# A hybrid HGRN2/GLA decoder step on one core: sample turns in one pass, squares added on VectorE, scaling in pieces, conditioning tiles in batches of eight, and an output stage on two engines

## What is computed

```python
def trunk(x, c, ...):
    cs = silu(c)
    for l in range(2):
        sh1, sc1, g1, sh2, sc2, g2 = split(cs @ w_ada[l] + b_ada[l], 6)   # conditioning
        h = x * (1 + sc1) + sh1
        y, s = (hgrn2_mixer if l == 0 else gla_mixer)(h, ...)
        x = layer_norm(ALPHA * x + (1 + g1) * y)
        h = x * (1 + sc2) + sh2
        y = square(relu(h @ w_up[l])) @ w_down[l]
        x = layer_norm(ALPHA * x + (1 + g2) * y)

def gla_mixer(h, ...):
    q, k, v, g, low = split(h @ w_in)
    log_f = log_sigmoid(low @ w_gk2 + b_gk) / 16
    o, s = gated_linear_recurrence(q * 256**-0.5, k, v, log_f, s0)
    o = o * rsqrt(mean(o * o) + eps) * norm_w * silu(g)      # per head of 512 values
    return o @ w_out, s
```

## Time and profile before

| | us |
|---|---|
| median of 3 runs (lowest, highest) | 3125.11 (3121.99, 3128.86) |
| the profiled execution's own time | 3127.16 |
| its span, first to last instruction | 3125.4 |
| PE busy | 3049.0 (98%) |
| DVE busy | 1734.8 (56%) |
| ACT busy | 1307.9 (42%) |
| POOL busy | 294.0 (9%) |

### The profile page before, as it was taken

One profiled execution on the slowest core, in us unless ns is written; L12 is line 12 of the kernel. 1 busy time (PEld: TensorE's weight loads), 2 busy tenths in 40 slices (PEclk: granted clock), 3 DMA queues, 4 the chain that ended last, 5 costly groups with the idle time before them and its releaser, 6 DMA issues.

```text
span 3125.4 us, 66220 instructions
## 1 busy us (share of the span) xinstructions
PE 3049.0 (98%) x26988; PEld 2852.2 (91%) x26988; DVE 1734.8 (56%) x2471; ACT 1307.9 (42%) x1702; POOL 294.0 (9%) x290
## 2 busy tenths in 40 slices
PE   6899999999999999999999999999999999999998
PEld 3689999989899999999999889997999999999998
DVE  2476776665744444444445666666574444454446
ACT  1355555553433333333333544544353343343433
POOL 0022111111300000000001401110130000000000
PEclk9899999999999999999999999999999999999999
DMA  9998788888777676776775875675545555555552
GB/s 376 317 309 258 252 258 261 269 287 278 259 252 236 209 254 212 229 241 205 238 254 176 266 233 169 197 235 184 162 135 164 168 164 168 163 167 165 166 167 73
DMA packets 541633, 685.60 MB, mean 219 GB/s; under 512 B 22225, under 2 KB 469257, under 8 KB 541065
## 3 DMA queue, kind: packets, MB, share of 16 engines
q1 hardware_dynamic: 484402, 625.43, 61.7%
q10 hardware_dynamic: 56960, 56.21, 5.5%
HBM read 650.88 MB, written 30.67 MB: 218 GB/s over the span
## 4 chain that ended last, share of the span: by engine, by line
PE 74%; DVE 3%; DMA 1%; ACT 1%; issue 0%; SPq 0%; DVEq 0%; ACTq 0%
PE main L560 23%; PE main L562 22%; PE main L561 22%; PE bank L572 2%; PE bank L1154 1%; PE bank L1139 0%; DMA raw<-in_w_ada 0%; DVE z L2404 0%; DVE z L2408 0%; PE bank L1125 0%; DVE w_lo L1905 0%; PE bank L702 0%; ACT w_hi L1291 0%; PE bank L1191 0%; DVE a_lo L2438 0%; PE bank L590 0%
## 5 line engine op out<-in xcount | busy, mean ns | idle before, releaser
L1905 DVE TENSOR_TENSOR w_lo<-raw,w_hi 128x1024 fp32r<-128x1024 f32 x804 | 988.2, 1231 | 1187.0 <-ACT w_hi L1291 1183.1
L1291 ACT ACTIVATE w_hi<-raw 128x1024 fp32r<-128x1024 f32 x804 | 850.3, 1059 | 1508.4 <-PE main L562 1394.4
L560 PE MATMUL main<-a_hi,w_hi 128*128 128x288 f32 x4224 | 1276.8, 302 | 8.7 <-DVE a_lo L2438 6.0
L562 PE MATMUL main<-a_hi,w_lo 128*128 128x288 f32 x4224 | 1248.5, 296 | 0.0
L561 PE MATMUL main<-a_lo,w_hi 128*128 128x288 f32 x4224 | 1247.4, 295 | 0.0
L560 PEld LDWEIGHTS main<-a_hi,w_hi 128*128 128x128 f32 x4224 | 796.2, 188 | 49.7 <-issue 35.2
L561 PEld LDWEIGHTS main<-a_lo,w_hi 128*128 128x128 f32 x4224 | 795.7, 188 | 4.6 <-issue 1.9
L562 PEld LDWEIGHTS main<-a_hi,w_lo 128*128 128x128 f32 x4224 | 795.8, 188 | 0.0
L560 PE MATMUL main<-act_hi,w_hi 128*128 128x288 f32 x2048 | 606.3, 296 | 0.0
L562 PE MATMUL main<-act_hi,w_lo 128*128 128x288 f32 x2048 | 604.9, 295 | 0.0
L561 PE MATMUL main<-act_lo,w_hi 128*128 128x288 f32 x2048 | 601.9, 294 | 0.0
(11 more groups left out here) (321 smaller groups left out, 2053.4 us busy)
## 6 DMA issues: line engine op xcount, KB each, us to landing
raw<-in_w_ada SPq DMA_DIRECT2D x384, 512.0 KB, 6.7
raw<-in_w_up SPq DMA_DIRECT2D x256, 512.0 KB, 3.8
raw<-in_w_down SPq DMA_DIRECT2D x256, 512.0 KB, 3.5
raw<-in_hg_w_in SPq DMA_DIRECT2D x128, 512.0 KB, 6.5
raw<-in_gla_w_in SPq DMA_DIRECT2D x100, 512.0 KB, 4.3
raw<-in_hg_w_out SPq DMA_DIRECT2D x32, 512.0 KB, 7.9
gl_s<-in_state_gla ACTq DMA_DIRECT2D x32, 512.0 KB, 5.7
out_new_gla_sample<-gl_s ACTq DMA_DIRECT2D x32, 512.0 KB, 4.8
```

Of the source, the lines that this page charges most:

```text
L560: mm(out, hi, x_hi[:, kb, :], start=kb == 0, stop=False)
L562: last = mm(out, lo, x_hi[:, kb, :], start=False, stop=kb == KB - 1)
L1291: F(w_hi[:, st.split_slot(g)].rearrange("p k n -> p (k n)"), raw[:, slot, :], ACT.Copy).then_inc(hi_ready, 1)
L1905: V.tensor_tensor(w_lo[:, s].rearrange("p k n -> p (k n)"), raw[:, slot, :], w_hi[:, s].rearrange("p k n -> p (k n)").bitcast(F32), ALU.su ...
```

## The change

It has six parts.

1. The samples are turned in one pass. The three copies that the strips need are made ahead (DVE's key product and ACT's value copy write three copies, `threefold`), and one true transpose of 96 columns replaces three products. The scores buffer grows from 64 to 96 rows to match.
2. In GLA, DVE adds the four blocks of squares (two additions), and PE sums one block and not four, at step 11 and not 10.
3. DVE's multiplication by the reciprocal root moves from step 10 to step 13, and the four by weight and gate to steps 14 to 17.
4. In MLP0 the 32 conditioning tiles of an iteration come in 4 batches of 8 and not in 8 of 4, in the first iteration at steps 8, 12, 24 and 36.
5. In GL0 the last 8 conditioning tiles come together ahead of step 9 and not as 4 ahead of step 3 and 4 ahead of step 6; the gate's two products move from steps 10 and 11 to 11 and 12, and the load of `w_gk2` no longer stands behind the conditioning copy on ACT.
6. At the end 8 banks are used, ACT and DVE share the copies, DVE applies weight and bias to the last chunk, and SP stores 9 of the 12 pieces.

In the piece with `if s == 10` the engine is DVE.

```diff
-    MLP_OPENING += [("a", i) for i in range(32) if step == max(6 * (i // 4), 3)] + first_weights(step + 3, min(step + 4, 64))
+    MLP_OPENING += [("a", i) for i in range(32) if step == max(12 * (i // 8), 8)] + first_weights(step + 3, min(step + 4, 64))
-MLP0 = Stage(HGO, 4, 64, {s: 4 for s in range(0, 48, 6)}, "A" * 8 + "V" * 8, lead=KB, opening=MLP_OPENING)
+MLP0 = Stage(HGO, 4, 64, {s: 8 for s in range(0, 48, 12)}, "A" * 8 + "V" * 8, lead=KB, opening=MLP_OPENING)
-GL0 = Stage(MLP0, 1, len(GL_FIRST), {0: 8, 3: 4, 6: 4}, emptied_by="AAAAVV")
+GL0 = Stage(MLP0, 1, len(GL_FIRST), {0: 8, 9: 8}, emptied_by="AAAAVV")
...
-        def turn_samples(bank, at, src, copies=3):
-            for j in range(copies):
-                last = mm(bank[32 * j:32 * j + 32, at:at + P], src, ident[:, :], start=True, stop=True,
-                          skip_group_check=True, tile_position=(0, 32 * j))
-            return last
+        def turn_samples(bank, at, src):
+            return turn(bank[0:96, at:at + P], src.rearrange("p c t -> p (c t)"), ident[:, :])
...
         def hg_key_mul(n):
             dve.wait_ge(H["kd_exp"], n + 1)
+            step(V.tensor_tensor(hg_s3[:, 2:4], threefold(hg["x"][:, 1, :, TP:T]), threefold(hg["k"][:, :, TP:T]), ALU.mult))
...
         def gl_sum(n):
-            pe.wait_ge(G["squared"], n + 1)
+            pe.wait_ge(G["sq_summed"], n + 1)
             pe.wait_ge(G["ss_read"], 8 * n + 8)
-            for v in range(4):
-                last = mm(b5[:, 0:T], ones[:, :], gl["v"][:, v, :], start=v == 0, stop=v == 3)
-            last.then_inc(G["summed"], 1)
+            mm(b5[:, 0:T], ones[:, :], gl["v"][:, 0, :], start=True, stop=True).then_inc(G["summed"], 1)
...
                 if s == 10:
-                    dve.wait_ge(G["rstd_ready"], pn + 1)
-                    o = o_buf[:, cols(4 * pn, 4), :]
-                    step(V.tensor_tensor(o, o, rstd[:, :].unsqueeze(1).to_broadcast([P, 4, T]), ALU.mult))
...
+                    dve.wait_ge(G["squared"], pn + 1)
+                    step(V.tensor_tensor(gl["v"][:, 0:2, :], gl["v"][:, 0:2, :], gl["v"][:, 2:4, :], ALU.add))
+                    V.tensor_tensor(gl["v"][:, 0, :], gl["v"][:, 0, :], gl["v"][:, 1, :], ALU.add).then_inc(G["sq_summed"], 1)
...
+            if prev:
+                if s == 13:
+                    gl_rstd_mul(pn)
+                elif 14 <= s <= 17:
+                    gl_scale(pn, s - 14)
...
+Y_COPIES = {"A": [0, 1, 2, 3, 4, 5, 8, 11], "V": [6, 7, 9, 10]}
+Y_STORES = [0, 1, 2, 3, 4, 6, 7, 9, 10]
```

More of the change, by code:

```diff
@@ L217, in __init__ @@
         self.top = nc.sbuf_usable_end
+        self.start = {}
     def put(self, name, shape, dtype=F32, at=None):
@@ L535, in _ @@
         mixer_stored(sp, G, GLA_HEADS * NB // 2, GLA_HEADS * 2)
+        for g in Y_STORES:
+            engine, count = y_copied(g)
+            sp.wait_ge(y_read[engine], count)
+            sp.dma_start(y_out(g), y_piece(g)).then_inc(y_stored, 16)
         sp.wait_ge(y_stored, 16 * 12)
@@ L1536, in hg_step @@
                     panel_done(HG, n, 11)
+                    F(hg_s3[:, 0:2], threefold(panel(HG, 2)[:, :, TP:T]), ACT.Copy)
                     F(hg["v"][:, :, :], panel(HG, 2), ACT.Copy).then_inc(panel_read["A"], 1)
@@ L1797, in gl_step @@
                     panel_done(GLA, n, s - 1)
+                    F(gl_sv[:, 2 * j:2 * j + 2], threefold(panel(GLA, 2 + j)[:, :, TP:T]), ACT.Copy)
                     F(gl["v"][:, 2 * j:2 * j + 2, :], panel(GLA, 2 + j), ACT.Copy).then_inc(panel_read["A"], 1)
@@ L1878, in _, with y_affine @@
         layer_norm(3, None)
-        for c in range(4):
+        def y_affine(c):
             act.wait_ge(ln_scaled, 5 * 3 + c + 1)
```

145 lines of the change are left out of this document (95 added, 50 removed).

## The result

The changed kernel takes 3105.18 us (median of 4 runs, 3104.58 to 3107.67), against 3124.98 us for the one before in the same comparison (4 runs, 3121.99 to 3128.86). The ratio is 0.9939, with a 95% interval from 0.9927 to 0.9951: 19.8 us less, with 3107.2 forecast. The profiled execution took 3104.89 us, its span is 3103.1 us, 22.3 us less than the one before.

The account below looks back on a forecast made before the run. PE, busy 98% of the span, was taken as the bound. Terms 7.7 + 3.5 - 1.5 + 4.8 + 2.1 + 1.3 = 17.9 us off the profiled 3127.16 gave 3109.3, less 2.05 to the median: 3107.2 us, range 3100 to 3118.

Parts of the forecast that it names:

- sample turns: In HG and GLA, fewer PE instructions to turn samples, less 0.4 us for DVE's extra copies: 7.7 us gained.
- squares: In GLA, six fewer PE instructions a head: 4.3 us gained in three heads, 0.8 us lost in GLO, 3.5 in all.
- the levels' delay: In GLA, scaling pieces on DVE make level products late: 0.5 us a head for three heads, 1.5 us lost.
- batches in MLP0: In MLP0, 32 conditioning batches become 16, each saving 0.3 us: 4.8 us gained.
- GL0: Gate waits of 2.8 us go, a new wait ahead of step 9 costs 0.7: 2.1 us gained.
- the end: At the kernel's end, PE's last turns, still at half clock, finish sooner: 1.3 us gained.
- Rival 3: Saved instructions come back as waits in HG, GL0's and the end's gains go too: 3114 to 3120 us, chance 0.08.
- following DVE from step 12 on with the durations of before: In GLA, level products of steps 13 and 15 come some 0.3 us late each, the others in time.
- Rival 1: In GLA's levels, moved scaling runs over twice its length beside POOL, PE waits 3 us more a head: 3115, chance 0.13.
- the ring's cover: In MLP0, weights are ready 6.7 us after the step, needed at 10.1: 3.4 us of cover, so loads stay hidden.
- landing 3.8 us later and multiplied, the batch ends at about 1756.2: In GL0, the last conditioning tile's load delays step 9 to about 1756.2, against 1755.45 before.
- Rival 2: In MLP0, the ring stalls on weight tile s+3 after each of 16 batches, kernel slower, 3136 at 9 us landings; chance 0.06.

Follow-up runs that it names:

- a_rows64: The changed kernel with the product of the samples' scores and the sample tile on 64 rows again in both mixers: 3110.18 us, ratio 0.9959.
- b_rows96: The kernel before with only the samples' scores on 96 rows and their product with the sample tile over 96 rows: 3118.97 us, ratio 0.9984.
- a_mlp4: The changed kernel with MLP0's conditioning tiles in batches of four again: 3111.04 us, ratio 0.9953.
- a_end_old: The changed kernel with the end as before: ACT scales all four chunks and issues all stores, DVE makes all twelve copies; 3107.25 us, ratio 0.9954 upper bound, 0.9940 itself.
- a_gl0_44: The changed kernel with GL0's conditioning tiles in two batches of four at steps 3 and 6 again, gate still late: 3096.49 us, ratio 0.9911.

## Why the prediction was right, and where it was not

The time and its sign were forecast rightly, within 2 us or so. That it came so near is luck: two steps were wrong, by +5 to +6 and by -4 us, and cancelled. Term by term, in us gained:

| term | forecast | measured | by |
|---|---|---|---|
| sample turns | 7.7 | 8.8 | HG 8 x 0.44 without the rows, GLA 4 x 1.32 |
| samples' product on 96 rows | not priced | 5.0 to 6.2 | a_rows64, b_rows96, 20 x 0.31 |
| squares | 3.5 | 3.9 | 3 x 1.44, less 0.44 in GLO |
| the levels' delay | -1.5 | -2.9 | 3 x 0.95, of it 3 x 0.33 the pieces |
| batches in MLP0 | 4.8 | 4.4 to 4.75 | a_mlp4, the table |
| GL0 | 2.1 | -2.1 | the table |
| the end | 1.3 | 1.3 | a_end_old |
| sum | 17.9 | 18 to 20 | measured 19.8 |

**Sample turns.** Right in size, 0.44 us a pair in HG where 0.45 was forecast before DVE's copy. The value turn of a GLA head with what stands round it takes 4.06 us and took 4.83, 0.77 us less (0.68 forecast), the key turn 0.55 (0.45). DVE's extra copy, for which the forecast took off 0.4 us in all, costs nothing that the trace shows: it is 0.36 us long in HG and 0.29 in GLA, and no wait of PE for it comes up. Rival 3, that the saved instructions come back as waits in HG, fell: from 194 us to the last sum PE waits 2.6 us before and 2.8 after.

**The unpriced edit.** This step was missing, and a term of 5 to 6 us stood at nothing without a reason. The forecast went through the changed instructions by kind and count, and this one keeps both. Only its shape changes.

**Squares.** Right in each part: 1.44 us a head, and in GLO a wait of 2.04 us against "about 2". The stretch there lost 0.44 us. The forecast has 0.8, but its own numbers, a wait of 2 less the 1.44, give under 0.6. GLO's other 1.2 us in the table are the clock's: its low stretch comes behind PE's long wait for `gl_ksm` before, and ahead of that wait in the changed kernel, where the wait takes it up.

**Scaling.** The sign was right, the size was not, and most of the mechanism was not either. The three delays of a head are 0.49, 0.13 and 0.33 us, 0.95 together, in place of 0.5. The forecast had the moved multiplications in the levels' way, and only the 0.33 us are theirs. The step that failed is "following DVE from step 12 on with the durations of before": the durations changed, because other instructions now run beside POOL's sums. The forecast had the row for it (1.19 us against 0.45) and the rule of the Trainium skill (SBUF — State Buffer, section "SBUF: two separate sides"), and applied them to the moved multiplications alone. The trace agrees with that rule in kind: the split takes 1.68 to 1.75 us beside POOL's sums and 1.21 to 1.23 without, and the multiplication by the root 1.82 against 1.36. Rival 1's price of 3 us a head is close to what PE waits with the block at step 11 (3.2 us), and the pieces avoid it.

**MLP0.** Right, and the ring's cover held.

**GL0.** The failed step is "landing 3.8 us later and multiplied, the batch ends at about 1756.2". The slots came free as forecast: DVE's split of tile 11 ends at 1736.9, 14.8 us before the 1751.7 named, and the run had gained 14.9 us by then. But the last three loads are issued at 1734.44, 1735.81 and 1736.94, each as a split frees its slot, with weight tiles right behind, and PE, waiting for each, uses them at 1738.26, 1740.73 and 1742.83: 3.8, 4.9 and 5.9 us later, with the DMA engines busy for 0.78 of the time and more. The price of one load issued alone was taken for the last of a queue, though the same group of rows had 7.0 us for such loads. The wait came out at 4.7 us, above the 2 to 4 that the forecast named. On top of it I had not reckoned with the clock, which falls to half while PE waits and stays there for 6.8 us. So a wait here costs more than its own length. Rival 2 had the right mechanism, a ring that stalls at a batch of eight, but its place was MLP0, where the cover held.

**The end.** The size was right, the reason half, so the size is partly luck. I had PE's last turns at half clock as the thing that ends last, 1.3 us sooner. They end 3.1 us sooner, and the stores behind them take 1.8 us more.

## What to carry to other kernels

Price a change of an instruction's shape, above all the number of rows or columns that it uses of the array, even where it only follows another edit: two changes of shape around a small product cost 0.31 us here, twenty times. For a batch of tiles in a ring as deep as the batch, ask when the slot of its last tile comes free and add the landing time of a load with others around it, and expect that a long wait on PE can also lower its clock behind it. Work moved off PE goes where its new engine has idle rows in the trace: 1.35 us on DVE cost 1.8 us a head in a stretch without gaps and nothing that could be measured seven steps later. And when work leaves a stretch, look at what now runs beside the other engines in its place: here the levels' own instructions became 1.8 us longer without a change to any of them.

## What the runs showed of the hardware

PE's granted clock falls to 0.50 in all these traces behind stretches in which PE waits, and a low stretch costs about half its length where PE is busy in it: the products of a step follow each other at 0.24 us in it and at 0.13 outside. Where PE then waits for another engine, the wait takes the loss up, as in GLO. Which of the short waits bring it down is not the same from one execution to the next: behind the same waits at the start of HGO it fell in the kernel before and in a_gl0_44, and not in the changed kernel nor in a_rows64. That alone moves a profile of this kernel by up to 1.7 us a place, which is why most terms under 2 us were read from stretches at the same clock and not from the medians.

The forecast used a rule of the Trainium skill (TensorE: Matmul & The Clock Gate, section "Part 4: PE-mode transpose") by which the turns at the end would stay at the lower level. The measurement decides against it as a rule: in the changed kernel PE runs nothing but turns from 3088 on, and the clock rises from 0.50 to 1.00 at 3096 with the last 16 recorded instructions still to come, and in a_gl0_44 all turns at the end run at 1.00, four of them in 0.66 us, as in this timeline:

```profile
3084.68 0.66 PE L1312 MATMUL main<-ident,z 128*128 128x128 f32 x4 [1.88 <-ACT z L1924]
3085.17 1.04 PE L1312 MATMUL bank<-ident,z 128*128 128x128 f32 x8
```

Even so that span ends 20.5 us after the normalisation's last product and the changed kernel's 20.9: the stores take most of what the clock gives.
